# A fused two-block forward pass: three groups of products computed with the weights stationary and the features on partitions, without the turns behind them

## What is computed

```python
def short_conv_mixer(h, w_in, w_conv, w_out):          # layer 0 only
    b_gate, c_gate, u = split(h @ w_in, 3)              # w_in 1024 x 3072
    z = c_gate * u
    conv = causal_depthwise_conv(z, w_conv)             # width 3, along the tokens
    return (b_gate * conv) @ w_out

def mem_cross_attention(h, mem_n, w_q, w_kv, w_o):      # both layers, 4 heads of 256
    q = h @ w_q
    k, v = split(mem_n @ w_kv, 2)
    p = softmax(q k^T / 16)                             # 256 memory rows
    return (p v) @ w_o

def swiglu(h, w_gu, w_down):                            # both layers, 2816 wide
    g, u = split(h @ w_gu, 2)
    return (silu(g) * u) @ w_down
```

## Time and profile before

| | |
|---|---|
| median of three runs | 1793.31 us |
| profiled execution | 1786.05 us |
| its span, first to last instruction | 1784.2 us |
| TensorE busy, weight loads busy | 1606.3 us (90%), 748.9 us (42%) |
| VectorE, ScalarE, GpSimd busy | 751.5, 501.2, 281.2 us |
| moved by DMA | 595.22 MB, mean 334 GB/s |
| end of the picks | 1296.7 us |

### The profile page before, as it was taken

The page is one execution under the profiler, slowest core; times in us unless marked ns, Lnnn a source line. Parts: engine busy times, 40 slices in busy tenths (PEclk is TensorE's granted clock), DMA queues, the critical chain, the costliest instruction groups (busy, mean ns, idle before and its releaser), DMA issues.

```text
span 1784.2 us, 15530 instructions
## 1 busy us (share of the span) xinstructions
PE 1606.3 (90%) x5460; PEld 748.9 (42%) x5460; DVE 751.5 (42%) x1808; ACT 501.2 (28%) x1283; POOL 281.2 (16%) x268
## 2 busy tenths in 40 slices
PE   6998988588659998699899997999999999999998
PEld 3444455154115353244344333343344544455443
DVE  3653036866586556655543446542212100031101
ACT  3311123322232223423344233334411210122210
POOL 1000001323232433412211222231100000000000
PEclk9998999799889999899999998999999999999999
DMA  9545146999999999999999999999977677765774
GB/s 355 197 171 189 78 194 259 404 376 414 422 413 359 395 422 421 421 414 417 404 422 421 420 421 422 395 422 421 409 272 265 236 295 286 302 236 224 282 286 185
DMA packets 94957, 595.22 MB, mean 334 GB/s; under 512 B 7024, under 2 KB 7024, under 8 KB 28192
## 3 DMA queue, kind: packets, MB, share of 16 engines
q1 hardware_dynamic: 56576, 319.28, 45.8%
q0 software_dynamic: 37584, 270.75, 37.0%
q10 hardware_dynamic: 720, 4.19, 0.6%
HBM read 593.15 MB, written 1.05 MB: 333 GB/s over the span
## 4 chain that ended last, share of the span: by engine, by line
PE 77%; DMA 13%; DVE 6%; ACT 2%; issue 2%; POOL 1%; SPq 0%; POOLq 0%; DVEq 0%; ACTq 0%
PE bank L965 35%; PE bank L1128 9%; DMA arena<-in_peer_rows,pidx 8%; PE bank L1043 8%; PE bank L675 7%; PE bank L937 3%; PE bank L928 3%; PE bank L752 3%; DMA ring<-in_w_mod 2%; PE bank L972 2%; DMA ring<-in_weights 2%; DVE arena L2063 1%; PE bank L729 1%; PE bank L1025 1%; PE bank L647 1%
## 5 line engine op out<-in xcount | busy, mean ns | idle before, releaser
L1601 POOL DMA_INDIRECT arena<-in_peer_rows,pidx x256 | 276.4, 1080 | 968.4 <-PE bank L1128 647.5
L2063 DVE SCALAR_TENSOR_TENSOR arena<-arena,ring 128x1024 f32<-128x1024 f32 x256 | 306.1, 1222 | 152.5 <-DMA arena<-in_peer_rows,pidx 151.3
L1128 PE MATMUL bank<-arena,keep 128*32 128x512 f32 x1024 | 266.2, 664 | 93.2 <-ACT keep L1559 93.1
L965 PE MATMUL bank<-ring,arena 128*128 128x512 f32 x736 | 319.4, 593 | 0.0
L965 PE MATMUL bank<-ring,hT_all 128*128 128x512 f32 x544 | 241.0, 599 | 3.4 <-issue 3.4
L965 PEld LDWEIGHTS bank<-ring,arena 128*128 128x128 f32 x736 | 138.5, 190 | 168.8 <-issue 168.7
L1128 PEld LDWEIGHTS bank<-arena,keep 128*32 128x32 f32 x1024 | 51.2, 116 | 257.2 <-issue 128.5
L965 PEld LDWEIGHTS bank<-ring,hT_all 128*128 128x128 f32 x544 | 101.8, 191 | 135.7 <-issue 135.7
L1546 ACT ACTIVATE pf<-pf 128x2 f32<-128x2 f32 x128 | 25.8, 202 | 374.7 <-DVE arena L2063 368.3
L2179 DVE TENSOR_TENSOR x_all<-x_all,bank 128x512 f32<-128x512 f32 x40 | 27.5, 688 | 202.5 <-PE bank L1043 107.4
L675 PE MATMUL bank<-ring,hT_all 128*128 128x512 f32 x192 | 89.3, 624 | 3.0 <-DVE hT_all L1678 3.0
(11 more groups left out here) (374 smaller groups left out, 1561.8 us busy)
## 6 DMA issues: line engine op xcount, KB each, us to landing
ring<-in_weights SPq DMA_DIRECT2D x126, 2048.0 KB
ring<-in_w_mod SPq DMA_DIRECT2D x12, 2048.0 KB
ring<-in_w_in SPq DMA_DIRECT2D x6, 2048.0 KB
ring<-in_weights SPq DMA_DIRECT2D x8, 1024.0 KB
arena<-in_peer_rows,pidx POOLq DMA_INDIRECT x256
ring<-in_weights SPq DMA_DIRECT2D x8, 512.0 KB
mem_all<-in_b_mod POOLq DMA_DIRECT2D x3, 512.0 KB, 9.6
hT_all<-in_xT ACTq DMA_DIRECT2D x1, 1024.0 KB, 6.6
```

Of the source, the lines that this page charges most:

```text
L965: m = mm(b[:, :], src[:, k], slot8[w][:, k], start=(k == 0), stop=(k == KC - 1))
L1128: m = mm(acc[b][r:r + 32, :], diag[n % 8], vslot[n % SLOTS][:, b * 512:(b + 1) * 512], start=(n % 128 < 4), stop=(n % 128 >= 124))
L1601: nc.gpsimd.indirect_dma_start(out=row_in[n % SLOTS], out_offset=None, in_=a["peer_rows"], in_offset=bass.IndirectOffsetOnAxis(ap=pidx[:, ...
L2063: stt(uslot[n % SLOTS], uslot[n % SLOTS], 1.0, h2g[n % 4], ALU.mult, ALU.mult, accum_out=pact2[:, 16 * (g % 2) + k:16 * (g % 2) + k + 1]). ...
```

## The change

For both tiles `turned_unit` takes the place of `layer_unit` in the convolution inputs ("cin"), the memory queries ("q") and the gate-and-up blocks ("gu"). A 128x128 part of the ring block is stationary and the 128 tokens of the turned activations move: 32 products of 128x128 by 128x128 in place of 8 of 128x128 by 128x512. The results come out with features on partitions, so "zturn", "bturn", "qturn" and "fturn" are gone.

With features on partitions, rs lies along the free axis. For the norms "conv", "ffn0" and "ffn1" a new step "spread" makes it a row on all partitions: VectorE builds diag(rs) from the identity, TensorE multiplies it by a matrix of ones, ScalarE copies the result. VectorE then multiplies the gate by this row before the silu, and by its square for z. The other factors of rs are applied where tokens lie on partitions again: when cout's and the down blocks' results are added to x, and for the memory attention in the softmax scale. The gate of the convolution ("gate") multiplies by ScalarE's copy of b in SBUF. TensorE waits for it through `tile_gated`. STEPS is now a list for each tile, and without the turns and their lags the planner reaches the last gate-and-up block at pick 240, where it was pick 250.

The core of the diff:

```diff
-    return [(f"turn mem{l}", 2, 2), (f"root mem{l}", 0, 0), (f"q{l} 0", 7, 2), (f"q{l} 1", 7, 0), (f"qturn{l} 0", 2, 2), (f"scores{l} 0", 4, 2),
+    return [(f"turn mem{l}", 2, 2), (f"root mem{l}", 0, 0), (f"q{l} 0", 7, 2), (f"q{l} 1", 7, 0), (f"scores{l} 0", 4, 2),
...
+def feed_steps(t, l):
 
     steps = [(f"turn ffn{l}", 2, 2), (f"root ffn{l}", 0, 0)]
     for j in range(11):
         steps.append((f"gu{l} {j}", 7, 0 if j else 2))
-        if j >= 2 and j % 2 == 0:
+        if t in TURNED_FEED and j == 0:
+            steps.append((f"spread ffn{l}", 0, 0))
+        if t not in TURNED_FEED and j >= 2 and j % 2 == 0:
             steps.append((f"fturn{l} {j // 2 - 1}", 1, 0))
-    return steps + [(f"fturn{l} 5", 1, 2)] + [(f"dn{l} {c}", 7, 0 if c else 2) for c in range(6)]
-
-
-STEPS = ([("turn conv", 2, 2), ("root conv", 0, 0), ("cin 2", 7, 2), ("cin 4", 7, 0), ("cin 3", 7, 0), ("cin 5", 7, 0), ("cin 0", 7, 0), ("zturn 0", 2, 0),
-          ("taps 0", 0, 0), ("cin 1", 7, 0), ("bturn 0", 2, 2), ("cout 0", 7, 2), ("cout 1", 7, 0)] + memory_steps(0) + feed_steps(0)
+    if t not in TURNED_FEED:
+        steps.append((f"fturn{l} 5", 1, 2))
+    return steps + [(f"dn{l} {c}", 7, 0 if c else 2) for c in range(6)]
...
 
                 tile_x_wait(pe, t, name, u)
 
-            def layer_unit(name, piece_of, src, low, high):
+            def turned_unit(name, piece_of, src, low, high):
 
                 w = weights(piece[piece_of])
                 unit_read(low)
                 b = open_unit(name)
+                for half in range(2):
+                    if half:
+                        unit_read(high)
+                    for c in range(4):
+                        for k in range(4 * half, 4 * half + 4):
+                            m = mm(b[:, c * P:(c + 1) * P], slot8[w][:, k, c * P:(c + 1) * P], src[:, k], start=(c == k == 0), stop=(c == 3 and k == KC - 1))
+                m.then_inc(unit_ready, 1)
+
+            def layer_unit(name, piece_of, src, low, high, t=None):
+
+                w = weights(piece[piece_of])
+                if t is None:
+                    unit_read(low)
+                else:
+                    pe.wait_ge(tile_gated[t], 1)
+                b = open_unit(name)
                 for k in range(KC):
-                    if k == 4:
+                    if k == 4 and t is None:
                         unit_read(high)
+                    elif k == 4:
+                        pe.wait_ge(tile_gated[t], 2)
                     m = mm(b[:, :], src[:, k], slot8[w][:, k], start=(k == 0), stop=(k == KC - 1))
...
-                    for u in range(2):
-                        unit_read(f"ci{t}{u}")
-                        layer_turns(f"b{t}{u}", [v.b_tok[:, (4 * u + c) * P:(4 * u + c + 1) * P] for c in range(4)])
+                    turned_unit(f"ci{t}{arg}", (f"cin{t}", int(arg)), v.hT, f"tconv{t}0", f"tconv{t}1")
+                elif kind == "spread":
+                    pe.wait_ge(tile_diag[t], spreads(t, arg) + 1)
+                    b = open_unit(f"rb{arg}{t}")
+                    mm(b[:, 0:P], v.ones[arg == "ffn1"], v.diag[arg == "ffn1"], start=True, stop=True).then_inc(unit_ready, 1)
                 elif kind == "cout":
-                    layer_unit(f"co{t}{arg}", (f"cout{t}", int(arg)), v.cvT, f"b{t}0", f"b{t}1")
+                    layer_unit(f"co{t}{arg}", (f"cout{t}", int(arg)), v.cvT, None, None, t)
                 elif kind == "q":
-                    layer_unit(f"lq{l}{t}{arg}", (f"q{l}{t}", int(arg)), v.hT, f"tmem{l}{t}0", f"tmem{l}{t}1")
-                elif kind == "qturn":
-                    for u in range(2):
-                        unit_read(f"lq{l}{t}{u}")
-                        layer_turns(f"qt{l}{t}{u}", [v.q_tok[:, (4 * u + c) * P:(4 * u + c + 1) * P] for c in range(4)])
+                    turned_unit(f"lq{l}{t}{arg}", (f"q{l}{t}", int(arg)), v.hT, f"tmem{l}{t}0", f"tmem{l}{t}1")
                 elif kind == "scores":
                     K = feat(mem[2 * l])
                     unit_read(f"mk{l}11")
                     for i in range(2):
-                        unit_read(f"qt{l}{t}{i}")
+                        unit_read(f"lq{l}{t}{i}")
                         b = open_unit(f"sc{l}{t}{i}")
                         for h in (2 * i, 2 * i + 1):
...
                     for k in ks:
-                        if half == 0 and k % 4 == 0:
+                        if half == 0 and t in TURNED_FEED and k % 2 == 0:
+                            unit_read(f"gu{l}{t}{k // 2}")
+                        elif half == 0 and t not in TURNED_FEED and k % 4 == 0:
...
+                elif kind == "spread" and arg == "conv":
+                    spread_copy("conv")
                 elif kind == "taps":
-                    act.wait_ge(unit_free["D"], units_freed(f"z{t}0", "D"))
-                    act.wait_ge(unit_free["A"], units_freed(f"z{t}1", "A"))
+                    act.wait_ge(unit_free["D"], units_freed(f"ci{t}5", "D"))
                     for c in range(KC):
                         f(v.cvT[:, c], v.zT[:, c, 0:P], ACT.Copy, scale=cols[:, C_CONV + c:C_CONV + c + 1]).then_inc(sem("tap0"), 1)
                 elif kind == "q":
-                    i, ss, ms, sd, rs = tile_stats(t, f"mem{l}")
-                    scaled(f"lq{l}{t}{arg}", v.q_tok[:, int(arg) * 512:(int(arg) + 1) * 512])
-                elif kind == "qturn":
-                    unit_copy(f"qt{l}{t}1", v.qT[:, 4:8])
+                    unit_copy(f"lq{l}{t}{arg}", v.qT[:, 4 * int(arg):4 * int(arg) + 4])
                 elif kind == "scores":
+                    scale = tile_stats(t, f"mem{l}")[2]
                     for i in range(2):
...
                     j = int(arg)
+                    if t in TURNED_FEED:
+                        if j == 0:
+                            spread_copy(f"ffn{l}")
+                        act.wait_ge(tile_gained[t], 11 * l + j + 1)
+                        f(v.sg[l][:, j % 2], v.sg[l][:, j % 2], ACT.Silu).then_inc(tile_silu[t], 1)
+                        return
                     act.wait_ge(unit_ready, unit(f"gu{l}{t}{j}") + 1)
...
+                    if arg == "conv" or arg[:3] == "ffn" and t == 0 and t in TURNED_FEED:
+                        nc.vector.memset(v.ones[arg == "ffn1"], 1.0)
+                    if arg == "conv" or arg[:3] == "ffn" and t in TURNED_FEED:
+                        dve.wait_ge(tile_rs[t], i + 1)
+                        ts(v.diag[arg == "ffn1"], ident, rs, None, ALU.mult).then_inc(tile_diag[t], 1)
                 elif kind == "final":
                     i, ss, ms, sd, rs = tile_stats(t, "final")
...
                     dve.wait_ge(sem("final_gained"), 2 * t + 2)
                     ts(high, high, rs, None, ALU.mult).then_inc(sem(f"tile{t}_done1"), 1)
+                elif kind == "spread" and arg == "conv":
+                    copied(f"rbconv{t}")
+                    link(tt(v.rows2, v.rows[0], v.rows[0], ALU.mult))
                 elif kind == "cin" and arg in "45":
-                    i, ss, ms, sd, rs = tile_stats(t, "conv")
                     u = int(arg) - 4
+                    if u == 0 and t == 0:
+                        link(nc.vector.memset(v.zT[:, :, 0:2], 0.0))
+                    elif u == 0:
+                        link(nc.vector.tensor_copy(v.zT[:, :, 0:2], ztail))
                     copied(f"ci{t}{2 + u}")
-                    dve.wait_ge(tile_rs[t], i + 1)
-                    part = v.z_tok[:, u * 512:(u + 1) * 512]
-                    stt(part, unit_in(f"ci{t}{arg}")[:, :], rs, part, ALU.mult, ALU.mult).then_inc(unit_free["D"], 1)
-                elif kind == "zturn":
-                    if t == 0:
-                        link(nc.vector.memset(v.zT[:, :, 0:2], 0.0))
...
                     for u in range(2):
-                        name = f"b{t}{u}"
-                        tt(v.cvT[:, 4 * u:4 * u + 4], v.cvT[:, 4 * u:4 * u + 4], unit_in(name)[:, :].rearrange("p (c n) -> p c n", c=4),
-                           ALU.mult).then_inc(unit_free["D"], 1)
+                        copied(f"ci{t}{u}")
+                        tt(v.cvT[:, 4 * u:4 * u + 4], v.cvT[:, 4 * u:4 * u + 4], v.b_tok[:, u * 512:(u + 1) * 512].rearrange("p (c n) -> p c n", c=4),
+                           ALU.mult).then_inc(tile_gated[t], 1)
                 elif kind in ("cout", "mo", "bo", "dn"):
                     half = int(arg) // (3 if kind == "dn" else 1)
                     name = {"cout": f"co{t}", "mo": f"lo{l}{t}", "bo": f"bo{t}", "dn": f"dn{l}{t}"}[kind] + arg
                     c = slice(half * 512, (half + 1) * 512)
                     if kind == "dn" and arg not in "03":
                         copied(f"dn{l}{t}{int(arg) - 1}")
-                    tt(x[:, t, c], x[:, t, c], unit_in(name)[:, :], ALU.add).then_inc(unit_free["D"], 1)
-                elif kind == "qturn":
-                    unit_copy(f"qt{l}{t}0", v.qT[:, 0:4])
```

(17 more changed lines are left out.)

55 lines of the change are left out of this document (29 added, 26 removed), and 2 rows, old and new, of the table late.

## The result

The changed kernel took 1806.46 us (median of six runs, 1802.95 to 1812.29), the kernel before 1788.51 us beside it (six runs, 1783.06 to 1794.34). The ratio is 1.0096, 95% interval 1.0076 to 1.0116: slower by some 17 us. The forecast was +3.8 us, no change to be seen. Its 1797 us was counted from 1793.31 us, the median of three runs of the kernel before; the median of six is 1788.51 us, so the two absolute numbers lie closer together than the two changes do.

A forecast was written before the change was run, and what follows sets the result against it. The prediction took bytes to bound the picks' stage and TensorE tile 1's part; -1.9 + 3 + 1.7 + 1 = +3.8 us on the 1793.31 us median gave 1797 us, range 1785 to 1812 us for 8 times in 10.

The forecast's parts named there:

- Tile 1's layers, -1.9 us: Tile 1's part after the picks: slower turned units and spreads against turns and waits removed, net -1.9 us.
- Rival C: All turned units: weight loads of 190 ns no longer hide and set the pace, about 2090 us; chance 0.02.
- TensorE's work up to the last unit, 508 us: Picks' stage: TensorE has 508 us of work up to pick 240.
- The 509 us of bytes: Picks' stage: the transfers needed up to pick 240 take 509 us, level with TensorE's work.
- The denser part in front of pick 240, +1 us: Tile 0's tighter steps: transfers run ahead while TensorE is late, so only +1 us, bounds -2 and +8.
- the lead of 35 us: Picks' stage: eight row slots and three ring slots hold 35 us of transfer, keeping the DMA going while TensorE is late.
- Rival B: Picks' stage: TensorE bounds up to pick 240, then a tail of picks; stage +12 us, 1805 us; most of 0.37 shared.
- The tail, +3 us (0 to +4.2): End of picks: 16 picks without layer work; last row at DMA rate, then dot, factors and a pair; +3 us.
- The clock, +1.7 us: After the light bare picks TensorE's granted clock is lower, slowing the first units behind; +1.7 us, bounds 0 and +3.6.
- D: Tile 1: removed turns' waits come back elsewhere, +3 in place of -1.9 us, 1802 us; shares 0.37, the smaller part.
- The sign that was named for B: Windows up to pick 240: a DMA share under 0.97 would mean TensorE had become the bound.
- TensorE busy throughout: Windows up to pick 240: TensorE always busy with full row slots would mean it had become the bound.

The follow-up runs named there:

- e4: Tile 0 as in the kernel before (wide units, turns, old picks), tile 1 turned as in the changed kernel; 1786.29 us, ratio 0.9983 to the kernel before.
- f1: Changed kernel with all steps from the turn of the shared keys on moved ten picks later, last gate-and-up block at pick 250; 1799.48 us.
- h1: Changed kernel with SyncE holding the block of tile 0's first last down block until the row of pick 254 has landed; 1807.71 us.
- e2: Changed kernel, turned units kept, each of tile 0's steps at its pick in the kernel before; 1793.29 us, ratio 1.0019 to that kernel.
- e3: Changed kernel with the planner's figure for a pick at 4.2 us in place of 5.2, last block at pick 252; 1785.02 us.
- light kernels: Changed kernel with a quarter of the products left out in 32 of tile 0's units (1798.69 us), or half in 46 (1788.44 us).
- g1: Changed kernel with half of the products left out in tile 0's 46 layer units, down blocks excepted; 1788.44 us.

## Why the prediction was wrong

1. *Tile 1's layers, -1.9 us*: right. A unit was put at 7.16 and takes 7.15 us; the spread 0.22 for 0.22; the covered waits are covered; -2.3 us in the profile. (The part takes 485.2 us, just under the 486 to 490 that the prediction named as its sign; 487.5 less 1.9 is 485.6.) e4, which has this part alone, is 2.4 us faster by its median; its ratio's interval, 0.9969 to 0.9998, leaves anything from 0.4 to 5.5 us.
2. *Rival C, loads no longer hidden*: wrong by the same rows. The loads last 192 ns and the matmuls begin every 7.15 / 64 = 0.112 us.
3. *TensorE's work up to the last unit, 508 us*: right (505.4). The 509 us of bytes that stood against it cannot be read off in the same way: 218 MB (535.5 us at 407 GB/s) had moved by the end of the last unit, the 212 of the sum and some of what came behind.
4. *The denser part in front of pick 240, +1 us*: this is the step that failed, by its argument. It set TensorE's 508 us of work against 509 us of bytes and let the lead of 35 us absorb the waits. TensorE's idle time did not shrink: 535.5 - 505.4 = 30.1 us, where it was 547.8 - 518.2 = 29.6 up to its own last unit. Rival B had put the arrival at 508 + 29.8 = 538 us; it was 535.5. The lead can't absorb a wait of TensorE itself: rows that are ahead don't make TensorE earlier, and only it frees the slots. Its premise, that in this part *the bytes set the end* and TensorE has 29.8 us to spare, is an average over the stage. From 1200 to 1280 us TensorE is busy without a break in both kernels (80.0 of 80 us), and in the kernel before the last row had landed at 1289.9 us by the trace's packets, 6.8 us before the end of the picks: there TensorE was the last already. That 30.1 and 29.6 agree so well is partly luck. In the other runs with all products in place the same idle time lies between 28 and 44 us (44.0 in f1).
5. *The tail, +3 us (0 to +4.2)*: failed with it. It took the rows to come in at the DMA's rate and added only dot, factors and a pair. With TensorE late, the last eight rows start only behind the last unit, as picks 240 to 247 are used, and the tail is 35.5 us. (The sum itself has a slip: 1294.8 + 2.30 + 1.4 + 1.91 or 3.63 is 1300.4 to 1302.1 us, not 1298.7 to 1300.9. It does not matter beside the end at 1316.0.)
6. *The clock, +1.7 us*: did not show behind the picks. The bare pairs run in part at the lower level (3.63 us appears again) but have 5 us each, and the first unit behind them takes 7.06 us, as before. In the bare picks the granted clock was 0.80 to 0.82, and 0.53 in the last 6 us; the last pair took 3.35 us where it took 1.91. Those 1.4 us are on the path, and the bounds of the tail had them.

So rival B was the right mechanism, held at 0.37 together with D. Its price, +12 us for the stage, was too small: 20 us for eight rows and 4 to 6 behind them against 35.5. Missing were the weight blocks that move among these rows (from 1280.5 to 1309.3 us some 11 MB moved, 8.4 of them rows) and the start of the gathers: GpSimd begins 2.6 us behind the last unit and issues the eight up to 13.2 us behind it, and four of the picks in front of them still wait some 5 us for VectorE, whose dots stand behind the last unit's product. h1 shows the sizes. Without the blocks the last row lands 26.0 us behind the last unit, with them 29.2 (by the packets): 3 us for the blocks, 6 us above the 20 for the start.

The sign that was named for B, a DMA share under 0.97 up to pick 240, would have missed it: the share was 1.00 (1.01 before) while the rate fell from 416 to 407 GB/s. The other one, TensorE busy throughout, tells nothing, since from 1200 to 1280 us it is so in both kernels.

**What stays open.** e2, with turned units at exactly the old picks, is 8 us slower than e3 (1.0019 against 0.9986, intervals apart), though by the sum TensorE's work grows by 1.8 us only; its last gather goes out at 1284.0 us, where it was 1275.8 in the kernel before. Its TensorE stood idle 552.6 - 514.0 = 38.6 us up to the last unit, and one wait for the factors of a pair took 8.2 us. Which step brings that wait was not tried. How much of the fall from 416 to 407 GB/s comes from late slots and how much from single queues (below) isn't separated either. Nor is the half of the loss that stays in the light kernels: the bytes fetched ahead account for it in g1, yet holding them back gave nothing in h1.

## What to carry to other kernels

Where gathers go through a fixed number of slots, find the use that frees the slot of the last gather, and count the other engine's work on both sides of it. Work before it delays the last transfers; only work behind it covers them. A planner that packs steps tighter because they became cheaper can turn the same work from cover into delay: after such a change its density (here one number, 5.2 against 4.2 us a pick, worth 21 us) has to be set again. And two engines that are "level" over a stage aren't a tie: the one whose idle time comes from dependences kept it in every run here with all products in place (28 to 44 us, 29.6 before), so compare its work plus today's idle time with the other's work, and look at the last stretch of the stage by itself.

## What the hardware showed that was not expected

*A queue that is alone loses its start.* Between two blocks on SyncE's queue, with no row in flight, the rate fell to 139 GB/s for 2 us. Windows of the changed kernel, around the release of a ring slot at 1047 us:

```profile
1043.00:1047.00 4.00, 4.00 (x10) 1.52 (x8) 0.00 (x0) 0.00 (x0) 0.00 (x0) 1.00 0.99 416
1047.00:1049.00 2.00, 2.00 (x10) 0.40 (x9) 0.00 (x0) 1.69 (x6) 0.00 (x0) 1.00 0.69 139
1049.00:1053.00 4.00, 4.00 (x13) 2.02 (x12) 3.29 (x9) 0.10 (x1) 2.25 (x2) 1.00 0.94 385
```

The Trainium skill (DMA: Bandwidth & Descriptors, "Anatomy of one DMA") puts a fixed cost of about 2.0 us on a transfer and describes it for GpSimd's path; this hole on SyncE's queue has that size. Counted by the trace's packets in half-microsecond steps of the picks' stage, the kernel before moves 420 GB/s with both queues busy and 393 with (next to) weights alone; the changed kernel spends 148 us with weights alone (389 GB/s) where it was 94, and with both queues busy it moves 413. A DMA share of 1.00 in a long window hides this; the GB/s beside it don't.
